# Attentions of a two-layer hybrid block: both heads of a pair in one step, scores in three passes of 64 rows

## The reference

```python
# first: causal, blocks of 128 queries, 8 heads
s = einsum('bqhd,bkhd->bhqk', q[:, q0:q0+128], k[:, :q0+128]) * 64 ** -0.5
s = s + cum[:, :, q0:q0+128, None] - cum[:, :, None, :q0+128]
s = where(k_pos <= q_pos, s, -1e30)
o = einsum('bhqk,bkhd->bqhd', softmax(s), v[:, :q0+128])
# second: chunks of 64 queries, the chunk and 8 chunks to its left, 4 heads
s = einsum('bcqhd,bckhd->bchqk', qc, kb) * 64 ** -0.5
s = where(valid, s + bias, -1e30)          # bias by clipped distance
o = einsum('bchqk,bckhd->bcqhd', softmax(s), vb)
```

## Time and profile before

| | us |
|---|---|
| median of three runs | 3460.83 |
| lowest and highest | 3458.84 and 3464.54 |
| the profiled execution, time | 3463.03 |
| the profiled execution, span of instructions | 3461.3 |
| PE busy | 3366.4 (97%) |
| DVE busy | 1311.0 (38%) |
| ACT busy | 944.6 (27%) |
| POOL busy | 940.3 (27%) |

### The profile page before, as it was taken

One profiled execution on the slowest core, in us unless ns is written; L12 is line 12 of the kernel. 1 busy time (PEld: TensorE's weight loads), 2 busy tenths in 40 slices (PEclk: granted clock), 3 DMA queues, 4 the chain that ended last, 5 costly groups with the idle time before them and its releaser, 6 DMA issues. The chain is left out here.

```text
span 3461.3 us, 40933 instructions
## 1 busy us (share of the span) xinstructions
PE 3366.4 (97%) x16184; PEld 2739.9 (79%) x16184; DVE 1311.0 (38%) x1631; ACT 944.6 (27%) x1248; POOL 940.3 (27%) x507
## 2 busy tenths in 40 slices
PE   8999999999999999999999999999999999999997
PEld 6788888777877888888867777787878688888886
DVE  6852455434244131313143427654461521121123
ACT  3213444444232111111233332313342411111112
POOL 2212222213332222222421124231254222122125
PEclk9999999999999999999999999999999999999998
DMA  3435444235411111111233222213362211111113
GB/s 129 159 94 159 129 151 149 95 115 184 146 63 65 49 49 49 48 49 47 93 125 118 96 101 101 80 68 144 136 213 97 79 48 49 48 48 49 49 52 130
DMA packets 101603, 333.43 MB, mean 96 GB/s; under 512 B 11920, under 2 KB 21520, under 8 KB 101328
## 3 DMA queue, kind: packets, MB, share of 16 engines
q1 hardware_dynamic: 100432, 327.95, 28.3%
q10 hardware_dynamic: 1040, 3.67, 0.3%
HBM read 249.06 MB, written 85.52 MB: 97 GB/s over the span
## 5 line engine op out<-in xcount | busy, mean ns | idle before, releaser
L282 POOL TENSOR_TENSOR w_lo<-w_raw,w_hi 128x1024 fp32r<-128x1024 f32 (+1 forms) x304 | 694.8, 2289 | 2348.8 <-ACT w_hi L278 2299.7
L322 PE MATMUL pair<-act_hi,w_hi 128*128 128x512 f32 x2976 | 942.8, 398 | 6.5 <-DVE f1v L2000 1.5
L322 PE MATMUL pair<-act_lo,w_hi 128*128 128x512 f32 x2976 | 920.9, 391 | 0.0
L322 PE MATMUL pair<-act_hi,w_lo 128*128 128x512 f32 x2976 | 919.6, 390 | 0.0
L322 PEld LDWEIGHTS pair<-act_hi,w_lo 128*128 128x128 f32 x2976 | 559.6, 188 | 119.8
L322 PEld LDWEIGHTS pair<-act_lo,w_hi 128*128 128x128 f32 x2976 | 559.6, 188 | 119.3
L322 PEld LDWEIGHTS pair<-act_hi,w_hi 128*128 128x128 f32 x2976 | 539.9, 189 | 111.9 <-issue 10.0
L278 ACT CAST w_hi<-w_raw 128x1024 fp32r<-128x1024 f32 x274 | 287.4, 1049 | 848.4 <-PE pair L322 802.2
L609 DVE TENSOR_TENSOR p<-pair,rs 128x1024 f32<-128x1024 f32 x100 | 122.2, 1222 | 406.4 <-PE pair L322 406.3
L1943 DVE TENSOR_TENSOR f2v<-pair,rs 128x1024 f32<-128x1024 f32 x42 | 51.4, 1225 | 333.1 <-PE pair L322 333.1
L322 PE MATMUL pair<-f1hl,w_hi 128*128 128x512 f32 x480 | 147.8, 389 | 0.0
(11 more groups left out here) (486 smaller groups left out, 4042.8 us busy)
## 6 DMA issues: line engine op xcount, KB each, us to landing
w_raw<-in_stream SPq DMA_DIRECT2D x275, 512.0 KB, 3.6
proj<-p SPq DMA_DIRECT2D x101, 512.0 KB, 2.6
m2g<-proj SPq DMA_DIRECT2D x32, 512.0 KB, 4.8
m1g<-proj SPq DMA_DIRECT2D x16, 512.0 KB, 3.5
x<-f1y SPq DMA_DIRECT2D x16, 512.0 KB, 2.6
act_lo<-x SPq DMA_DIRECT2D x16, 512.0 KB, 6.9
foxx<-proj SPq DMA_DIRECT2D x28, 256.0 KB, 5.7
fx_cb<-fox_cum SPq DMA_DIRECT2D x8, 512.0 KB, 7.5
```

Of the source, the lines that this page charges most:

```text
L282: last = nc.gpsimd.tensor_tensor(wlo[:, slot, at:at + n], raw[:, slot, at:at + n], whi[:, slot, at:at + n].bitcast(F32), ALU.subtract)
L322: last = nc.tensor.matmul(out_pair[:, h * HALF:(h + 1) * HALF], wt, a[:, h * HALF:(h + 1) * HALF], start=k == 0 and n_pass == 0, stop=k == ...
```

## The change

One step is now one (pair i, block n) for both heads. q and k are loaded once per pair (one DMA of 512 KB each, 128 partitions), and `high` and `low` hold the split q and k of two pairs. `scores` makes three passes (high x high, high x low, low x high) whose contraction has 64 rows; successive matmuls alternate between the heads, head 0 on partitions 0 to 63 and head 1 on 64 to 127, into different banks of `wide`. Each head now has 512 columns of `wide`, so blocks of more than 512 keys take a second call, `scores(i, n, HALF)`, after the second transposes group of the step. The transposes of step t - 1 stand in step t, in two or four groups, and background points behind each (six or eight points per step); `weigh` of step t - 1 stands at the end of step t, right ahead of the next step's scores. `s` has two buffers per head. `values` stands at the end of n == 0. Ahead of the first scores stands only `point(5)`; the points in all are 57 per pair + 13, that is 241 and 127.

In `fox`, `own` holds the rows of both heads, loaded by DMAs of their own and masked in place on POOL; in `band` the four heads' biases are loaded at the start, and `edges(0)` adds the edge mask to two heads in one DVE instruction, emitted in `first()`, ahead of `prepare`. What is removed stands in the code above. The added lines, cut:

```diff
             raw_qk, raw_v = sb(at, name + "x", [P, 2, L]), sb(at, name + "v", [P, L])
-            qh, ql, ks = (sb(at, name + n, [P, 2, L], F32R) for n in ("qh", "ql", "ks"))
+            high, low = (sb(at, name + n, [P, 2, 2, L], F32R) for n in ("h", "l"))
...
+            bias_first, bias_ahead, add_bias = head_bias(at)
+            s, pt = sb(at, name + "s", [P, 2, 2, L]), sb(at, name + "pt", [P, 2, NT, P])
+            o, st = sb(at, name + "o", [P, L]), sb(at, name + "st", [P, 2, 2, 2])
...
+                    arrived[i] = qk_in[i % 2].mark(queue.dma_start(raw_qk[:, n, :], src[i + rows[n]]))
+                if i:
+                    SP.wait_ge(*v_read[i - 1])
+                v_in.mark(queue.dma_start(raw_v[:], src[i + rows[2]]))
+            def prepare(i, n):
+                hi, lo = high[:, i % 2, n, :], low[:, i % 2, n, :]
+                a = A.mark(A.after(arrived[i], scored.get(i - 2)).copy(hi, raw_qk[:, n, :]))
+                split[i, n] = V.mark(V.after(a).tensor_tensor(lo, raw_qk[:, n, :], hi.bitcast(F32), ALU.subtract))
...
+                w = min(HALF, k1 - k0 - c)
+                PE.after(split[i, 1], state["scores_read"])
+                for q, k in ((high, high), (high, low), (low, high)):
+                    for x in range(2):
+                        head = slice(x * HD, (x + 1) * HD)
+                        last = nc.tensor.matmul(wide[:, x * HALF:x * HALF + w], q[head, i % 2, 0, q0:q0 + P],
+                                                k[head, i % 2, 1, k0 + c:k0 + c + w], start=q is high and k is high,
+                                                stop=q is low)
+                scored[i] = ready = PE.mark(last)
+                for x in range(2):
+                    state["scores_read"] = add_bias(i, n, x, c, c + w, s[:, t % 2, x, :], wide[:, x * HALF:x * HALF + w],
+                                                    V.after(ready, turned.get(t - 2), *(settled if t < 2 else ())))
+            def turn(t, x, j0, m, ready):
+                PE.after(ready[x], state["bank"], *(settled if t == 0 else ()))
+                for j in range(m):
+                    last = nc.tensor.transpose(bank[0][:, j * P:(j + 1) * P], s[:, t % 2, x, (j0 + j) * P:(j0 + j + 1) * P],
+                                               ident[:])
+                turned[t] = PE.mark(last)
+                state["bank"] = A.mark(A.after(turned[t]).copy(
+                    pt[:, x, j0:j0 + m, :], bank[0][:, 0:m * P].rearrange("p (j n) -> p j n", j=m)))
+            def weigh(i, n):
+                q0, k0, k1 = tiles[n]
+                nk = (k1 - k0) // P
+                PE.after(state["bank"], copied[i], state["o_read"])
                 for j in range(nk):
+                    for x in range(2):
+                        head = slice(x * HD, (x + 1) * HD)
+                        last = nc.tensor.matmul(bank[1][head, n % 4 * P:(n % 4 + 1) * P], vt[:, k0 // P + j, head],
+                                                pt[:, x, j, :], start=j == 0, stop=j == nk - 1)
+                weighed[i] = PE.mark(last)
...
             fetch(0)
+            bias_first()
             point(5)
+            prepare(0, 0)
+            prepare(0, 1)
+            before, ready = None, None
+            for t, (i, n) in enumerate((i, n) for i in range(pairs) for n in range(NT)):
...
+                w, total = k1 - k0, 8 if k1 - k0 > HALF else 6
                 if n == 0:
...
+                scores(i, n, 0)
+                parts = groups(before[1]) if before else [None, None]
+                exps = {}
+                for g, part in enumerate(parts):
+                    if part:
+                        turn(t - 1, *part, ready)
+                    if g == 1 and w > HALF:
+                        scores(i, n, HALF)
+                    if g == (2 if len(parts) == 4 else int(w > HALF)):
+                        for x in range(2):
+                            sc, sm = s[:, t % 2, x, 0:w], st[:, t % 2, x, 0:1]
+                            V.mark(V.then().reduce_max(sm, sc, AX.X))
+                            exps[x] = V.mark(V.then().tensor_scalar(sm, sm, -1.0, None, ALU.mult))
+                        exps[0] = A.mark(A.after(exps[0]).activation(s[:, t % 2, 0, 0:w], s[:, t % 2, 0, 0:w], ACT.Exp,
+                                                                     bias=st[:, t % 2, 0, 0:1],
+                                                                     accum_out=st[:, t % 2, 0, 1:2]))
+                        next(aside, None)
+                    point(total / len(parts))
+                if before:
+                    weigh(*before)
+                if n == 0:
+                    values(i)
+                exps[1] = A.mark(A.after(exps[1]).activation(s[:, t % 2, 1, 0:w], s[:, t % 2, 1, 0:w], ACT.Exp,
+                                                             bias=st[:, t % 2, 1, 0:1], accum_out=st[:, t % 2, 1, 1:2]))
+                ready = []
+                for x in range(2):
+                    sm = st[:, t % 2, x, 1:2]
+                    v = V.mark(V.after(exps[x]).reciprocal(sm, sm))
+                    ready.append(A.mark(A.after(v).activation(s[:, t % 2, x, 0:w], s[:, t % 2, x, 0:w], ACT.Copy, scale=sm)))
+                if before:
+                    gather(*before)
                 next(aside, None)
-            turn(*ready_p)
-            gather(*ready_p[0:3])
-            ready_p = (*exped[:-1], scaled(*exped))
-            point(1)
-            turn(*ready_p)
-            gather(*ready_p[0:3])
+                bias_ahead(i, n)
+                if n == 2 and i + 1 < pairs:
+                    fetch(i + 1)
+                if n in (4, 5) and i + 1 < pairs:
+                    prepare(i + 1, n - 4)
+                before = i, n
+            for part in groups(before[1]):
+                turn(t, *part, ready)
+                point(2)
+            weigh(*before)
+            gather(*before)
...
+            def first():
+                own_rows(0, 0, slice(0, (NT - 1) * P))
+                own_rows(0, 1, edge)
+                rows(0)
+                mask(0, 0)
+            def ahead(i, n):
+                if n == 0 and i:
+                    SP.wait_ge(*read[i - 1, NT - 1, 1])
+                    own_rows(i, 1, edge)
+                    rows(i)
+                if n < NT - 1:
+                    mask(i, n + 1)
+                elif i + 1 < pairs:
+                    SP.wait_ge(*read[i, NT - 2, 1])
+                    own_rows(i + 1, 0, slice(0, (NT - 1) * P))
+                    mask(i + 1, 0)
...
+                def edges(i):
+                    whole[i] = V.mark(V.after(here[i], edged).tensor_tensor(
+                        rel[:, i, :, :], rel[:, i, :, :], edge[:].unsqueeze(1).to_broadcast([P, 2, BAND]), ALU.add))
+                def first():
+                    for i in range(pairs):
+                        for x in range(2):
+                            here[i] = bias_load[i].mark(SP.dma_start(rel[:, i, x, :], t["rel"][2 * i + x]))
+                    edges(0)
+                def ahead(i, n):
+                    if n == 5 and i + 1 < pairs:
+                        edges(i + 1)
+                def add(i, n, x, c, e, sc, psum, vector):
+                    off = max(0, LEFT - n * P) + c
+                    return V.mark(V.after(whole[i]).scalar_tensor_tensor(
+                        sc[:, c:e], psum, HD ** -0.5, rel[:, i, x, off:off + e - c], ALU.mult, ALU.add))
...
-            w.again(FOX_HEADS * 28 + 11, 2 * KT)
+            w.again(FOX_HEADS // 2 * 57 + 13, 2 * KT)
...
-                w.again(BAND_HEADS * 28 + 12, 32 * KT)
+                w.again(BAND_HEADS // 2 * 57 + 13, 32 * KT)
```

More of the change, by code:

```diff
@@ L1 @@
+import itertools
 import math
@@ L689, in short_conv, with attention @@
         return beside
-    def attention(heads, tiles, src, rows, stored, mixed, row0, head_bias, add_bias, name, beside, first_queue=nc.sync):
+    def attention(pairs, tiles, src, rows, stored, mixed, row0, head_bias, name, beside, first_queue=nc.sync):
         entered, settled = [x.last() for x in (V, A, G, PE, load, store, *loads)], [x.last() for x in stores]
@@ L801, in attention, with groups @@
+            def groups(n):
+                q0, k0, k1 = tiles[n]
+                nk = (k1 - k0) // P
+                return [(x, j0, min(4, nk - j0)) for x in range(2) for j0 in range(0, nk, 4)]
             fetch(0)
+            bias_first()
             point(5)
-            prepare_q(0)
-            prepare_k(0)
-            point(3)
-            exped, ready_p = None, None
-            for t, (h, n) in enumerate((h, n) for h in range(heads) for n in range(NT)):
+            prepare(0, 0)
@@ L815, in attention @@
-                for c in range(0, w, HALF):
-                    e = min(w, c + HALF)
-                    for q in (qh, ql):
-                        last = nc.tensor.matmul(wide[:, c:e], q[:, h % 2, q0:q0 + P], ks[:, h % 2, k0 + c:k0 + e],
```

(24 more changed lines are left out.)

179 lines of the change are left out of this document (41 added, 138 removed).

## The result

The changed kernel takes 3482.24 us (median of 4 runs, 3480.5 to 3485.64) against 3461.73 for the kernel before in the same session (4 runs, 3458.84 to 3464.54): ratio 1.0061, 95% interval 1.0045 to 1.0077. It is slower, by 20.5 us; 17.6 were predicted, and the range held.

What follows compares the result with a forecast made beforehand. PE's matmul stream was taken to bound the kernel; +5.2 stream, +4.2 and +8.5 starts, +2.2 clock, -11.2 old stalls, +8.7 new gave +17.6, so 3478.4 us; main case 3469 to 3488, range 3463 to 3498.

Steps and rivals of the forecast that it cites:

- PE's stream (columns, switches): Matmuls of both attentions: fewer score columns save 11.6 us, switches into and out of 64-row mode cost 16.8, together +5.2.
- start of the first attention: Before the first scores: background tiles end 5.45 us earlier, PE waits for the split of k, +4.2 us.
- clock behind it: PE's clock falls behind the long first wait: +2.2 us in the first attention; the second pays that already.
- start of the second: Second attention's first scores wait 12.1 us for rel rows, `edges(0)` on DVE and the splits, 8.5 us more than before.
- old stalls: In both attentions all of PE's old idle time but the second start's 3.65 us is gone: -11.2 us.
- stalls at `values` and the step behind: New waits at n == 0 for copies of v and scaling of head 0, 7.2 us, plus 1.5 chance meetings: +8.7.
- rival B: Score matmuls: the two halves do not overlap in F32R, 34.8 us more on PE, 3513 us; chance 0.06.
- rival A: 64-row score groups: mode switches cost nothing, -16.8 us, so 3461.6, within 0.2% of before; chance 0.13.
- Rival C: Second score parts wait for the first part's additions on busy DVE, 18 us more, 3496 us; chance 0.13.
- Rival D: New starts cost little and removed stalls count fully: 3457 us at best; chance 0.10 with any faster mix.
- the new DMAs of the first attention are hidden: First attention's rows and own rows per pair, issued a step ahead, cost PE no wait.
- May land up to 1 us earlier: First attention's start: two loads of 512 KB instead of four of 256 KB may land up to 1 us earlier.

Runs made afterwards that it cites:

- the two passes: The changed kernel with scores as two passes of 128 rows per head instead of three of 64 rows for both: 3476.83 us, ratio 1.0042.
- the fastest kernel: Changed kernel with bias rows issued early, edge mask behind the splits, point(3) back, and a background tile behind each half of `values`: 3453.08 us, ratio 0.9968.
- the three edits alone: Changed kernel with bias rows issued at the start of their step, edge mask behind the splits and point(3) put back: 3457.24 us, ratio 0.9986.
- the repaired version: Changed kernel with bias rows early, edge mask behind splits, point(3) back: 3457.24 us; with a background tile behind each half of `values` too: 3453.08 us.

## Why the prediction held, step by step

The found values are differences between the two profiled executions (spans 3461.3 and 3483.8 us).

| step | predicted | found | from |
|---|---|---|---|
| PE's stream (columns, switches) | +5.2 | +1.1 | PE's work at full clock in the two attentions, 705.4 and 706.6 (1.1 before rounding) |
| start of the first attention | +4.2 | +0.5 | a wait of 0.50 against none |
| clock behind it | +2.2 | 0 | no stretch at half speed there |
| start of the second | +8.5 | +6.5 | wait 10.10 against 3.65 |
| clock behind it | 0 | -0.7 | 2.1 us lost against 2.8 |
| old stalls | -11.2 | -11.2 | PE's idle times of before, without that start |
| stalls at `values` and the step behind | +8.7 | +7.0 | PE's other idle times after |
| waits for the bias rows | 0 | +8.2 | three waits ahead of weigh |
| clock behind them | 0 | +4.8 | three stretches of 3.4 us at half speed, less what PE idled in them |
| sum for the two attentions | +17.6 | +16.2 | |
| outside the attentions | 0 | +6.3 | 6.1 of it clock |
| sum | +17.6 | +22.5 | medians of the runs: +20.5 |

**Right, and shown by runs.** The halves overlap: rival B fell, and the run on the same half paid its price. The switches have the prices that the half-array groups of before showed: rival A fell, and the run with a tile between paid 0.21 for each added trip. The second start is held by the rows of `edges(0)` and the early end of the background tiles, both with their share. Rival C did not come: the largest wait of scores for additions is 0.12 us. Rival D was half right: the first start costs next to nothing and the old stalls are gone, but not the rest.

**Wrong: "the new DMAs of the first attention are hidden".** The prediction looked at when they are issued in the program, a step ahead, and at POOL behind them. It did not look at SP's queue in front of them, where `gather`'s store of the pair before holds them until the last result is there; then they take 5.8 us to land, and DVE, ACT's exponential, ACT's copy and PE stand one behind the other. It cost 15.4 us by the run that moves them.

**Wrong in size: the stream.** The mechanism is as predicted, but the sum is not: +1.1 us against the kernel before and +3.5 against the two passes in the same order of work, instead of +5.2. By the distances in the trace the switches cost some 18 us (46 steps to transposes at 0.16, 24 second parts at some 0.45), near the predicted 16.8, and the columns saved 11.6. What the prediction left out is that the scores of before were not free either, some 0.03 us at each of 94 places between scores and background, 3 us. The remaining 2 to 3 us are not explained.

**Wrong: the start of the first attention.** "May land up to 1 us earlier" was 3.2 us (306.0 against 309.2). The attention began 0.85 us earlier, and from the first issue to the first cast it took 5.93 us instead of 8.27. The run with four loads took 8.27 again, so the number of DMAs is the cause of these 2.3 us.

The terms that were too high are 14.4 us together (the stream 4.1, the first start with its clock 5.9, the second 2.7, the stalls at `values` 1.7), the missed one is 13.0. So the forecast of the total was better than its parts, and that is luck. The 6.3 us outside the attentions belong to no step of the change: the runs behind the medians have no traces, and in other profiled executions that part was smaller. The interval of the ratio alone is 11 us wide.

What stays open: these 2 to 3 us of the stream, and why a stretch at half speed comes in some executions and not in others outside the attentions. One wait of 2.45 us ahead of weigh at 568.54 remains in the fastest kernel. Its trace shows the same kind of chain: the load `cvc` of the convolution, issued at 556.41, lets DVE go on at 562.87 only, and the additions, the exponential, a cast and the copy stand behind it. With the three edits alone DVE went on 5.6 us after that issue instead of 6.5, and the wait was 0.23. No run moves this load.

## What to carry to other kernels

Where a step is merged or moved, walk each DMA it issues back along the queue that issues it: the DMA is as late as whatever stands in front of it there waits, and here bias rows behind a store cost 15.4 us, more than the 11.6 us of columns that the change saved. Count half-array matmuls by slots, two halves in one, and add some 0.1 us each for entering, leaving and the first uncovered load: three passes of 64 rows for two heads paid in the first part of long blocks (0.90 against 1.05 us) and not over all steps. Where a few us decide, compare the work of the bounding engine at full clock in the traces, since times of equal stages moved by as much with the clock. After a regrouping, put background work back ahead of each new first wait before judging it; the repaired version beat both kernels while the plain one lost 0.6%.

## What the runs showed of the hardware that was not expected

- Matmuls on different halves of the rows need not alternate in the program: with three of one half ahead of three of the other they start in pairs 0.23 us apart all the same, and the time is unchanged (3481.41 against 3482.24 us). The Trainium skill's page TensorE: Matmul & The Clock Gate (The mechanism, in the part on packing small matmuls) has matmuls start in strict program order; the starts in this trace differ, and for the two halves the trace decides. Whether they also end out of order is not shown, since ends are modelled.
- In the first attention of the changed kernel, waits of PE of 2.59 to 3.00 us were each followed, within 2.3 us, by 3.4 us at half the clock (around the 2.85 us one of the run with four loads it was 6.8 us). The waits of 0.50 to 0.82 us there had no such stretch beside them, but for two that stood within 2 us of a long one. The fastest kernel had 3.4 us at half the clock beside its wait of 2.45 us.
- Two subtractions of 1024 columns on DVE took 2.35 us alone and 4.50 beside one on POOL; the edge mask of 1280 columns took 1.49 and 3.66.
